# Final RMSNorm of a streaming encoder: gain multiplied in on TensorE, its last outputs shared by two engines

## What is computed

```python
def swiglu(x, w_gu, w_dn):
    g, u = jnp.split(x @ w_gu, 2, axis=-1)
    return (jax.nn.silu(g) * u) @ w_dn

def rmsnorm(x, g):
    xf = x.astype(jnp.float32)
    y = xf * lax.rsqrt(jnp.mean(xf * xf, axis=-1, keepdims=True) + EPS)
    return (y * g.astype(jnp.float32)).astype(x.dtype)

h = h + swiglu(rmsnorm(h, norm_ffn[l]), w_gate_up[l], w_down[l])
y = rmsnorm(h, g_final)
```

## Time and profile before

| | |
|---|---|
| median of 3 runs | 2611.77 us |
| the profiled execution, its own time | 2613.04 us |
| its span, first to last instruction | 2611.3 us |
| PE busy | 2575.4 us, 99% |
| DVE, ACT, POOL busy | 42%, 26%, 26% |
| mean granted TensorE clock | 0.996 |

### The profile page before, as it was taken

The page is one execution under the profiler, slowest core; times in us unless marked ns, Lnnn a source line. Parts: engine busy times, 40 slices in busy tenths (PEclk is TensorE's granted clock), DMA queues, the critical chain, the costliest instruction groups (busy, mean ns, idle before and its releaser), DMA issues. The chain is left out here.

```text
span 2611.3 us, 37891 instructions
## 1 busy us (share of the span) xinstructions
PE 2575.4 (99%) x15296; PEld 2511.1 (96%) x15296; DVE 1107.2 (42%) x2301; ACT 673.1 (26%) x1474; POOL 675.1 (26%) x641
## 2 busy tenths in 40 slices
PE   8999999999999999999999999999999999999998
PEld 7999999999999999999999988899999999999998
DVE  6444464254323333332338656655333233333334
ACT  5222233142111111111115555534111111111112
POOL 1322222212221211122126343434121112211114
PEclk9999999999999999999999999999999999999999
DMA  4445555111111111111112234011111111111111
GB/s 148 142 133 143 166 172 165 49 33 41 49 41 41 42 41 48 33 49 41 41 61 42 55 81 119 18 41 49 41 43 42 46 33 49 44 42 45 41 41 73
DMA packets 244240, 171.23 MB, mean 66 GB/s; under 512 B 47352, under 2 KB 232876, under 8 KB 244036
## 3 DMA queue, kind: packets, MB, share of 16 engines
q1 hardware_dynamic: 243876, 168.78, 22.2%
q10 hardware_dynamic: 192, 0.04, 0.0%
HBM read 136.99 MB, written 33.59 MB: 65 GB/s over the span
## 5 line engine op out<-in xcount | busy, mean ns | idle before, releaser
L197 POOL TENSOR_TENSOR wl<-raw,wh 128x512 fp32r<-128x512 f32 x264 | 337.6, 1303 | 1288.4 <-ACT wh L189 1288.4
L349 PE MATMUL psum<-xh,wl 128*128 128x400 f32 (+1 forms) x1872 | 430.1, 338 | 0.0
L349 PE MATMUL psum<-xl,wh 128*128 128x400 f32 (+1 forms) x1872 | 428.5, 337 | 0.0
L349 PE MATMUL psum<-xh,wh 128*128 128x400 f32 (+1 forms) x1872 | 427.3, 336 | 0.0
L477 DVE TENSOR_TENSOR h<-h,psum 128x384 f32<-128x384 f32 (+1 forms) x528 | 265.0, 553 | 280.0 <-PE psum L369 267.2
L349 PEld LDWEIGHTS psum<-xh,wl 128*128 128x128 f32 x1872 | 336.7, 188 | 0.0
L349 PEld LDWEIGHTS psum<-xl,wh 128*128 128x128 f32 x1872 | 336.6, 188 | 0.0
L349 PEld LDWEIGHTS psum<-xh,wh 128*128 128x128 f32 x1872 | 335.9, 188 | 0.0
L2201 PE MATMUL psum<-xh,wh 128*128 128x384 f32 (+1 forms) x792 | 276.6, 349 | 8.0 <-DVE h L2373 4.8
L2201 PE MATMUL psum<-xl,wh 128*128 128x384 f32 (+1 forms) x792 | 272.2, 344 | 0.0
L2201 PE MATMUL psum<-xh,wl 128*128 128x384 f32 (+1 forms) x792 | 270.9, 342 | 0.0
(11 more groups left out here) (248 smaller groups left out, 3698.0 us busy)
## 6 DMA issues: line engine op xcount, KB each, us to landing
raw<-in_w_gate_up SPq DMA_DIRECT2D x88, 512.0 KB, 3.9
raw<-in_w_down SPq DMA_DIRECT2D x44, 512.0 KB, 3.5
raw<-in_a_w_in SPq DMA_DIRECT2D x24, 512.0 KB, 4.8
fr_qkv<-qkv_d SPq DMA_DIRECT2D x36, 256.0 KB, 3.8
qkv_d<-fr_tmp SPq DMA_DIRECT2D x32, 192.0 KB, 2.0
hn_d<-fr_hn_turned SPq DMA_DIRECT2D x36, 128.0 KB, 3.3
fr_xin<-in_x_prompt SPq DMA_DIRECT2D x8, 512.0 KB, 5.3
fr_decode_state<-in_state_c SPq DMA_DIRECT2D x4, 1024.0 KB, 7.2
```

What stands on the lines that cost most here:

```text
L197: pool.tensor_tensor(wl[:, self.slot(p), v], raw[:, self.raw_of(p), v], wh[:, self.slot(p), v].bitcast(F32), ALU.subtract).then_inc(self.w ...
L349: y = pe.matmul(psum[:, bank + c, 0:nt], w[:, k, :], x[:, k, t0:t0 + nt], start=(k == 0 and m == 0), stop=(k == KD - 1 and m == 2))
```

## The change

1. g_final is loaded with the other gains (a seventh row group of 8 rows by one more DMA of ACT, so that L2278 turns 88 rows), and the broadcast load of fi_gain is gone.
2. ACT makes eight diagonal matrices ident * g_final, 128x128 each, ahead of its squares.
3. turn(u) is a matmul of h with these diagonals instead of a transpose with the identity: the gain is then in the bank. normal(u) is a tensor_scalar with 1/rms alone.
4. After the last down group PE runs turns 12, 14 and 16 first (they need h blocks 0 to 3 only), then totals(2), then 13, 15 and 17.
5. For chunk 2 POOL makes six additions instead of seven; the last square is summed by three more matmuls, which accumulate in totals(2).
6. Of the last six outputs DVE makes 12, 14, 16, and ACT 13, 15, 17 (an activation Copy with scale). ACT issues the last store itself.

```diff
-    gains = sb("gains", [P, 6, KD])
+    gains = sb("gains", [P, 7, KD])
@@ class Final, __init__
-        self.gain, place = at("fi_gain", [P, D], F32, f1.end)
+        self.scaled, place = at("fi_gain_diagonal", [P, KD, P], F32, f1.end)
-        self.gl, self.gl0 = m.tab_ld, 32
+        self.dg, self.dg0 = m.tab_ld, 32
+        self.ev_act, self.ev_act0 = m.neg, 2 * NSTEP
+    ORDER = (12, 14, 16, 13, 15, 17)
+
     def bank(self, u):
-        if u < 12:
-            return 7 - u % 2
-        return u - 11 if u < 17 else 7
-
-    def sync(self, sp):
-        sp.dma_start(self.gain[:], self.a["g_final"].rearrange("(a d) -> a d", a=1).to_broadcast([P, D])).then_inc(self.gl, 16)
+        return 7 - u % 2 if u < 12 else (3, 4, 5, 1, 2, 7)[self.ORDER.index(u)]
@@ store
-        for u in range(18):
+        for u in range(17):
-            sp.wait_ge(self.ev, self.ev0 + u + 1)
+            if u < 12 or u % 2 == 0:
+                sp.wait_ge(self.ev, self.ev0 + (u + 1 if u < 12 else u // 2 + 7))
+            else:
+                sp.wait_ge(self.ev_act, self.ev_act0 + u // 2 - 5)
@@ scalar
         f1 = self.f1
+        for k in range(KD):
+            act.activation(self.scaled[:, k, :], self.ident[:], ACT.Copy, scale=self.s["gains"][:, 6, k:k + 1])\
+                .then_inc(self.dg, 1)
...
+        for u in (13, 15, 17):
+            i, half = u // 2, u % 2
+            w = slice(512 * half, 512 * half + 512)
+            act.wait_ge(self.turned, self.turned0 + self.ORDER.index(u) + 13)
+            act.wait_ge(self.rs, self.rs0 + 3)
+            act.wait_ge(self.sto[i % 3], self.sto0[i % 3] + 32 * (i // 3))
+            act.activation(self.y[:, i % 3, w], self.psum[:, self.bank(u), :], ACT.Copy,
+                           scale=self.ss[:, 2, 1, i % 3:i % 3 + 1]).then_inc(self.ev_act, 1)
+        act.wait_ge(self.ev_act, self.ev_act0 + 3)
+        act.dma_start(self.a["y_s"].rearrange("b t d -> (b t) d")[:, 512:D], self.y[:, 2, 512:D]).then_inc(self.sto[2], 16)
@@ gpsimd
-            for k in range(1, KD):
+            for k in range(1, KD if c < 2 else KD - 1):
@@ totals
-        pe.wait_ge(self.added, self.added0 + 7 * c + 7)
+        pe.wait_ge(self.added, self.added0 + 7 * c + (7 if c < 2 else 6))
...
             pe.wait_ge(self.f1.dn_evac, self.f1.after["dn_evac"])
+            pe.wait_ge(self.sqr, self.sqr0 + 24)
         for i in range(3):
-            x = pe.matmul(self.psum[:, 6 if c < 2 else 0, i:i + 1], self.acc[:, t0 + P * i:t0 + P * i + P], self.ones[:, 0:1],
-                          start=True, stop=True)
+            out = self.psum[:, 6 if c < 2 else 0, i:i + 1]
+            x = pe.matmul(out, self.acc[:, t0 + P * i:t0 + P * i + P], self.ones[:, 0:1], start=True, stop=(c < 2))
+            if c == 2:
+                x = pe.matmul(out, self.sq[:, 0, P * i:P * i + P], self.ones[:, 0:1], start=False, stop=True)
@@ turn
+        if u == 0:
+            pe.wait_ge(self.dg, self.dg0 + KD)
...
-            x = pe.transpose(self.psum[:, self.bank(u), k * P:(k + 1) * P],
-                             self.h[:, 4 * half + k, META + i * P:META + (i + 1) * P], self.ident[:])
+            x = pe.matmul(self.psum[:, self.bank(u), k * P:(k + 1) * P],
+                          self.h[:, 4 * half + k, META + i * P:META + (i + 1) * P], self.scaled[:, 4 * half + k, :],
+                          start=True, stop=True)
@@ tensor
+        pe.wait_ge(self.f1.dn_evac, self.f1.after["dn_evac"] - 3)
+        for u in self.ORDER[:3]:
+            self.turn(pe, u)
         self.totals(pe, 2)
-        for u in range(12, 18):
+        for u in self.ORDER[3:]:
             self.turn(pe, u)
@@ normal
-        dve.scalar_tensor_tensor(self.y[:, i % 3, w], self.psum[:, self.bank(u), :], self.ss[:, i // 3, 1, i % 3:i % 3 + 1],
-                                 self.gain[:, w], ALU.mult, ALU.mult).then_inc(self.ev, 1)
+        dve.tensor_scalar(self.y[:, i % 3, w], self.psum[:, self.bank(u), :], self.ss[:, i // 3, 1, i % 3:i % 3 + 1], None,
+                          ALU.mult).then_inc(self.ev, 1)
@@ vector
-        for u in range(12, 18):
+        for u in range(12, 18, 2):
             self.normal(dve, u)
@@ the program's own lists
-            fin.sync(sp)
...
-                                   a["norm_mix"][1], a["norm_ffn"][1])):
+                                   a["norm_mix"][1], a["norm_ffn"][1], a["g_final"])):
...
-            pe.wait_ge(gl, 112)
+            pe.wait_ge(gl, 128)
```

More of the change, by code:

```diff
@@ L1539, in normal @@
         w = slice(512 * half, 512 * half + 512)
-        dve.wait_ge(self.gl, self.gl0 + 16)
-        dve.wait_ge(self.turned, self.turned0 + u + 1)
+        dve.wait_ge(self.turned, self.turned0 + (u if u < 12 else 12 + self.ORDER.index(u)) + 1)
         dve.wait_ge(self.rs, self.rs0 + i // 3 + 1)
@@ L1582, in front @@
     dgt, _ = at("fr_diag", [P, 4, P], F32, place[0])
-    grow, _ = at("fr_small_rows", [6 * KD + NB * HA, P], F32, place[0] + 4 * P * 4)
+    grow, _ = at("fr_small_rows", [7 * KD + NB * HA, P], F32, place[0] + 4 * P * 4)
     hnc = sb("hn_loaded", [P, 2, CW])
@@ L1898, in _ @@
             for n, g in enumerate((a["norm_mix"][0], a["a_g_head"][0], a["norm_ffn"][0], a["g_kv"],
-                                   a["norm_mix"][1], a["norm_ffn"][1])):
+                                   a["norm_mix"][1], a["norm_ffn"][1], a["g_final"])):
                 act.dma_start(grow[KD * n:KD * n + KD, :], g.rearrange("(k p) -> k p", p=P)).then_inc(gl, 16)
-            act.dma_start(grow[6 * KD:6 * KD + NB * HA, :], a["state_n"].rearrange("b a h d -> (b a h) d")).then_inc(gl, 16)
+            act.dma_start(grow[7 * KD:7 * KD + NB * HA, :], a["state_n"].rearrange("b a h d -> (b a h) d")).then_inc(gl, 16)
             with nc.allow_non_contiguous_dma("small"):
@@ L2275, in seq_updates @@
                     pe.matmul(psum[:, bank, 0:E1], kwm[rows, b % 2, :], va[rows, 1, :], start=True, stop=True).then_inc(csp, 1)
-            pe.wait_ge(gl, 112)
-            pe.transpose(psum[:, UB, 0:6 * KD + NB * HA], grow[:], ident[0:6 * KD + NB * HA, 0:6 * KD + NB * HA]).then_inc(grt, 1)
+            pe.wait_ge(gl, 128)
+            pe.transpose(psum[:, UB, 0:7 * KD + NB * HA], grow[:], ident[0:7 * KD + NB * HA, 0:7 * KD + NB * HA]).then_inc(grt, 1)
             turn_x(0)
@@ L2515, in _ @@
             dve.wait_ge(grt, 1)
-            dve.tensor_copy(gains[:].rearrange("p n k -> p (n k)"), psum[:, UB, 0:6 * KD]).then_inc(gnd, 1)
-            dve.tensor_copy(n_in[:].rearrange("p b h -> p (b h)"), psum[:, UB, 6 * KD:6 * KD + NB * HA]).then_inc(gnd, 1)
+            dve.tensor_copy(gains[:].rearrange("p n k -> p (n k)"), psum[:, UB, 0:7 * KD]).then_inc(gnd, 1)
+            dve.tensor_copy(n_in[:].rearrange("p b h -> p (b h)"), psum[:, UB, 7 * KD:7 * KD + NB * HA]).then_inc(gnd, 1)
             place_x(0)
```

## The result

The changed kernel takes 2621.01 us (median of 7 runs, 2619.04 to 2621.9) against 2611.73 us (7 runs) for the kernel before on the same chip: the ratio is 1.0034 with a 95% interval of 1.0024 to 1.0044. A second measurement, on another occasion, gave 2619.74 against 2610.81 us, ratio 1.0030 (1.0019 to 1.0042). The forecast was 2619.7.

What follows compares the result with a forecast made beforehand. The prediction took TensorE, busy for 99% of the span, as the bound. Its terms 5.0 + 1.26 + 1.45 + 0.2 made +7.9 us on 2611.8, so 2619.7 us, 0.30% slower, with a range of 2616.3 to 2622.9.

Steps and rivals of the forecast that it cites:

- Turns between the down groups: TensorE's eleven turns 0 to 10: eight instructions instead of four, each turn 0.92 us instead of 0.463, +5.0 us.
- The page's "4× faster for FP32": Rival for TensorE's turns: a product costs four transposes, 0.45 us, a turn 1.8 us; 2633.6 us, chance 0.03.
- Diagonals: ACT's eight diagonal matrices ahead of its squares delay POOL's additions and totals(0): +1.26 us (1.0 to 1.9).
- The clock at totals(0): Rival: TensorE's longer pause before totals(0) brings 3.4 us at half clock, costing 1.7 us; 2621.4 us, chance 0.17.
- Tail: From turn 11 to the end: first output later, six stores at full rate set the end, +1.45 us.
- DVE's outputs: DVE's outputs read one operand fewer, but DVE has slack, so worth nothing.
- Start: One more 4 KB DMA on ACT's queue ahead of state_n at the kernel's start: +0.2 us (0 to +0.4).
- the first rival: The granted clock falls to half behind TensorE's pause before totals(0), costing 1.7 us; 2621.4 us, chance 0.17.

Runs made afterwards that it cites:

- e1_transposes: Changed kernel with its turns as transposes against the identity again, diagonals kept, g_final missing from y; 2613.22 us, ratio 1.0007 to the kernel before.
- e3_fill: Changed kernel with twelve additional transposes of the identity in TensorE's pause ahead of totals(0); 2618.45 us, ratio 1.0028 to the kernel before.
- e7_start: Kernel before with only the small loads of the change, g_final as a seventh row group; 2611.26 against 2610.81 us, ratio 1.0001.

## Why the prediction was right, point by point

- **Turns between the down groups (+5.0).** The step was the count of instructions, two for a product and one for a transpose, at one distance. Measured: 4.87 us in e1_transposes, and 4.88 from e3_fill's 25.02 against the 20.14 of the first trace before, both at full clock; 0.44 per turn, so each instruction at 0.11. It was the largest term and the surest, because other lines of the same trace already had the same shape.
- **The page's "4× faster for FP32"** (the Trainium skill, "TensorE: Matmul & The Clock Gate", section Terms), read as the ratio of a product to a transpose, would have given 1.8 us for a turn. The runs show 0.89 for a turn of products and 0.46 for one of transposes, a ratio of 1.9. The measurement decides against 4 for this form.
- **Diagonals (+1.26).** Measured +1.07. Eight took 2.44 us as estimated, and POOL began 0.59 behind the square of k = 1, but that square came 0.15 earlier behind ffn_hidh than reckoned, and POOL's seven additions took 7.98 us instead of 8.01.
- **The clock at totals(0)** was a rival with 0.17 and not a term of the sum. That is where the prediction was too low: the pause of 1.55 us was followed by 3.4 us of half clock in five of six traces that have it, at a cost of 1.6 us. I held it unlikely because the pause would be shorter than the one of its kind that I had, 1.75 against 1.83 us, and at another moment. It came out 0.2 us shorter still, and the clock fell all the same. The kernel before and e7_start, which have the pause of 1.83 us at totals(2), show half clock behind it in three of four traces.
- **Tail (+1.45).** Measured +1.59 against a trace of before with full clock in the tail, +1.23 against the first. All its steps are in the trace: totals(2) 3.41 us behind D (expected, from D, about 3.5), the sums 1.4 us, ACT's output 0.69 (0.67), the stores at full rate. The first output starts 6.03 us behind D where 6.39 were expected. The step that the tail hangs on first output and stores, and not on the last output, was right: the 1.59 us are the first output's, and the halved stores show the limit. The +1.45 was reckoned from a trace whose totals(2) ran at half clock, 1.18 us from its start to the means instead of 0.87. The note that the six instructions at half clock last as long as twelve at full came out as 1.18 against 1.44 us, up to the means. The text's own 14.7 against 13.2 us makes +1.5.
- **DVE's outputs (0).** The tensor_scalar takes 0.74 us, the scalar_tensor_tensor took 0.745: one operand fewer is worth nothing.
- **Start (+0.2).** e7_start measures +0.45 us with an interval of -2.1 to +2.6, and the traces differ by up to 2.2 us there among themselves. The term can't be told from nothing.

The sum of the terms was 7.9, and 9.3 were measured. The half clock (+1.6) was left out, turns and diagonals were 0.1 and 0.2 too high, and the tail 0.1 too low. What happened is the first rival's case, and its 2621.4 us is nearer to the 2621.0 measured than the forecast's 2619.7: the direction and the large terms were reasoned, the course of the clock was called the less likely way. The low end of the range, 2616.3, has no working; the lowest terms give 2617.1.

## What to carry to other kernels

Folding a factor into an f32 transpose turned one TensorE instruction into two here; do it where TensorE waits, not where it is the chain. Before moving work into a pause, compare its length with the pause and ask who waits for what stands behind it. Where stores at full rate end the kernel, ask when the first output is ready, not the last. And a small job put ahead of a chain on a half-idle engine can cost twice if that chain ends in a pause of TensorE: once as time, once as clock; here the same job, earlier in that engine's list, cost nothing that the trace shows.

## What I had not expected of the hardware

- Twelve transposes that compute nothing, in a pause of 1.57 us, went with a granted clock of 1.00 and a stage 1.59 us shorter, in one trace. In the earlier trace rows the clock rose from 0.50 to 1.00 behind a stretch that held the sums of totals(2) and otherwise transposes alone. The Trainium skill, "TensorE: Matmul & The Clock Gate", section "Part 4: PE-mode transpose", says that the full clock doesn't engage for transposes. These f32 transposes, with the clock at 1.00 through and behind them, don't bear that out.
- The same program's traces differ in the stretch of half clock near 17 us (3.4 or 6.8 us), and by 2.2 us in the time up to the last down groups. With differences of a few microseconds, the stages of two traces must be compared from a common point, not from the start of the span.
